# Gates of a PEER layer: one-hot products on TensorE, or a scatter into device memory and a multiply on VectorE

## The chip, the cores and the metric

One core of a Trainium2 chip runs the whole program in one launch. The metric is device time in microseconds from start to end of that launch; lower is better. The engines are TensorE (PE; PEld is its weight load), VectorE (DVE), ScalarE (ACT), GpSimd (POOL) and SyncE (SP), which issues most DMAs. A trailing q (SPq, POOLq) is an engine's own queue of instructions.

## What is computed

A decoder trunk of two layers over 256 tokens of width 1024. Layer 0 is a Mamba2-SSD mixer and then a PEER block, layer 1 an HGRN2 mixer and then a PEER block, with RMSNorms before each and at the end. The change is in the PEER block:

```python
def one_block(xb):                          # 128 tokens
    q = (xb @ w_query).reshape(nb, 8, 2, 128)
    sc = jnp.einsum('nhcd,hckd->nhck', q, sub_keys)
    top_s, top_i = lax.top_k(sc, 16)        # per head and half
    ...
    best_s, best_pos = lax.top_k(cand_s, 16)
    idx = jnp.take_along_axis(cand_i, best_pos, axis=-1)
    gate = jax.nn.softmax(best_s, axis=-1)
    u, v = expert_u[idx], expert_v[idx]
    act = jax.nn.gelu(jnp.einsum('nhkd,nd->nhk', u, xb), approximate=False)
    return jnp.einsum('nhk,nhkd->nd', gate * act, v)
```

There are 16384 experts, numbered i x 128 + j. Each token picks 16 of them for each of 8 heads, and the same expert may be picked by two heads of a token.

## The kernel before

Neither kernel gathers experts. Each streams all 16384 rows of expert_u and expert_v through TensorE, 128 experts a tile, in 128 tiles of 512 KB for u and 128 for v. The activations of all experts for all 256 tokens are kept in SBUF (`big`: 128 x 128 x 256), and a gate that is zero for experts not picked is multiplied in between u and v.

A stream of tiles runs through all stages of the program (ssd_in, ssd_z, ssd_out, q0, u0, v0, hgrn_in, hgrn_out, q1, u1, v1). For each tile SP loads `raw` into one of four buffers, ACT rounds it to `whi` (L465), POOL or VectorE makes the rest `wlo` = raw - whi, and TensorE multiplies hi by hi, hi by lo and lo by hi. In u (L783, `project`) these are 24 matmuls of 256 columns a tile, and ACT's Gelu moves the result to `big` (L711). In v (L1114, `contract`) they are 12 matmuls of 512 columns; the activations are split in the same way, by ACT into `hhi` (L747) and by POOL into `hlo` (L453), two tiles ahead. Before the change POOL makes `wlo` in the q and u stages (L424) and VectorE in v (L1712).

During the u stage VectorE makes the lists (L1607 to L1660): for two blocks of 128 tokens it finds the top 16 of each half, head by head, then of the 256 sums (`cand`, L1629), turns positions into indices i and j (L1648, L1652, L1655), and subtracts the best score. ACT takes the exponential, VectorE divides by the sum.

Then comes the gate stage, after the last u tile and before the first v tile. Indices were written as 7 bits of +1 and -1 plus a bias row, sent through device memory to be turned (`feat`, `feat_rows`), and multiplied with a matrix of signs (L1075, `matches`): a sum is positive only where i or j agrees. ACT and VectorE turn the sums into one-hot rows (`oha`, L736; `ohb`, weighted by the gate, L1698 and L741), TensorE multiplies them for each token (L1094), which gives the 128 x 128 table of gates of that token, and VectorE multiplies eight tokens' tables into `big` (L1689). 32 such rounds make a layer. `clear` (L819) writes zeros to the four banks in which v accumulates.

The order on each engine is that of the code. All waits are on semaphores: ACT's split of tile g waits until TensorE is done with tile g - 4, SP's load waits until `wlo` of the tile four before is made, and TensorE waits for both parts of a tile. The loads of v's tiles after the second wait for the end of the gate stage, since `ohb` lies in `raw`.

Of the kernel before, what the change touches and what calls it, by code (L numbers as in the profile page):

```python
# [28 lines left out]
P = 128  # L29
# [17 lines left out]
BITS = 7  # L47
FEAT = BITS + 1

# [4 lines left out]

ON_DVE = ("ssd_in", "hgrn_in", "hgrn_out", "v0", "v1")
# [5 lines left out]
for _n, _c in STREAM:  # L61
    FIRST[_n], POOL_LO[_n], DVE_LO[_n], EVAC[_n] = _g, _p, _d, _e
    _g += _c
    if _n in ON_DVE:
        _d += _c
    else:
        _p += _c
    if _n not in ("ssd_out", "v0", "v1"):
        _e += _c
# [33 lines left out]
LISTS_AT = 24  # L103


def trunk(nc, x_t, par, con, w_dt, weights, sub_keys, out_t):
# [11 lines left out]
    with ctx:  # L118
# [12 lines left out]
        zero = sb("zero", [P, 512], mybir.dt.bfloat16)  # L131
        gate_t = sb("gate_t", [P, T])
        signs = sb("signs", [P, 16, P], BF16)
# [22 lines left out]
        def norm_bank(n):  # L156
# [15 lines left out]
        ones_set = sem("ones_set")  # L172

# [71 lines left out]
        gate_v = sem("gate_v")  # L245
        lt_mm = sem("lt_mm")
        lt_v = sem("lt_v")
        oha_done = sem("oha_done")
        ohb_done = sem("ohb_done")
        ohb_act = sem("ohb_act")  # L250
        xa_mm = sem("xa_mm")
        xb_mm = sem("xb_mm")
        signs_mm = sem("signs_mm")
        signs_v = sem("signs_v")
        feat_v = sem("feat_v")
        feat_out = sem("feat_out")
        feat_in = sem("feat_in")
        gate_mm = sem("gate_mm")
# [68 lines left out]
        oha = [hhi[:, 2 * r:2 * r + 2, :].rearrange("p a (b k) -> p (a b) k", k=P) for r in range(4)]  # L327
        ohb = [raw[:, 2 + r, :, :] for r in range(2)]
        whole = work(26112, 512, 4).bitcast(U32)
        feat = work(26624, 2048).bitcast(BF16).rearrange("p (c f k) -> p c f k", c=4, f=FEAT)  # L330
        feat_rows = small[:, :, :].rearrange("p a b -> p (a b)").bitcast(BF16) \
            .rearrange("p (s k) -> p s k", s=32)
        feat_out_t = [nc.dram_tensor(f"feat{n}", [4, P, FEAT, P], BF16).ap() for n in range(2)]

# [13 lines left out]
        def rounds(eng, name, body, first=True, last=False):  # L348

            n = COUNT[name] // RAW  # L350
            a, b = int(first), n - int(last)
            if first:
                body(0)
            if b > a:
                with eng.Fori(a, b) as i:
                    body(i)
            if last:
                body(n - 1)

# [3 lines left out]
        def _(sp):  # L363
# [5 lines left out]
            sp.dma_start(tri, con[CON["tri"]]).then_inc(tri_in, 16)  # L369

# [7 lines left out]

            prev = None
            for name in STAGES:  # L380
                lo, at = (lo_dve, DVE_LO) if name in ON_DVE else (lo_pool, POOL_LO)
# [5 lines left out]
                def body(i):  # L387
                    for r in range(RAW):
                        if isinstance(i, int) and i == 0:
                            before = None  # L390
                            if prev is not None:
                                plo, pat = (lo_dve, DVE_LO) if prev in ON_DVE else (lo_pool, POOL_LO)
                                before = plo, pat[prev] + COUNT[prev] - RAW + r + 1
                            if name[0] == "v" and r == 2:

                                sp.wait_ge(gate_mm, 32 * int(name[1]) + 32)
                        else:
                            before = lo, at[name] + RAW * i + r - RAW + 1
                        load(name, i, r, before)
                if name == "hgrn_in":  # L400

                    body(0)
                    sp.wait_ge(x_done, 8)
                    sp.dma_start(lev, con[CON["lev"]:NCON].rearrange("n p q -> p n q")).then_inc(lev_in, 16)
                    with sp.Fori(1, COUNT[name] // RAW) as i:
                        body(i)
                else:
                    rounds(sp, name, body)
                prev = name
# [7 lines left out]
        def _(pool):  # L417
# [9 lines left out]
            def los(name, a=0):  # L427
                with pool.Fori(a, COUNT[name] // RAW) as i:  # L428
                    for r in range(RAW):
                        lo(name, i, r)  # L430

            for layer in range(2):
                if layer == 0:
                    los("ssd_z")
                    los("ssd_out")
# [7 lines left out]
                los(f"q{layer}")  # L443
                los(f"u{layer}")
# [14 lines left out]
        def _(act):  # L459
# [161 lines left out]
            for layer in range(2):  # L621
# [90 lines left out]
                stream(f"u{layer}", gelu, 0, SCRATCH0 // RAW)  # L712

                act.wait_ge(lists, 2 * layer + 2)
                nc.scalar.activation(lst[:, 2, :], lst[:, 2, :], ACT.Exp).then_inc(gexp, 1)
                nc.scalar.preload_act_table(ACT.Gelu)
                act.wait_ge(feat_v, layer + 1)
                act.dma_start(feat_out_t[layer].rearrange("c t f k -> t c f k"), feat).then_inc(feat_out, 16)
                stream(f"u{layer}", gelu, SCRATCH0 // RAW, 26)

                act.wait_ge(lt_v, layer + 1)
                act.wait_ge(feat_out, 16 * layer + 16)
                for c in range(2):
                    act.dma_start(feat_rows[64 * c:64 * c + 64], feat_out_t[layer][2 * c:2 * c + 2]
                                  .rearrange("b (s t) f k -> (t f) (b s) k", t=8)).then_inc(feat_in, 16)
                stream(f"u{layer}", gelu, 26)

                for m in range(32):  # L730
                    if m >= 2:

                        act.wait_ge(gate_mm, 32 * layer + m - 1)
                    for q in range(2):
                        act.wait_ge(xa_mm, 64 * layer + 2 * m + q + 1)
                        nc.scalar.activation(oha[2 * (m % 2) + q], bank[4 + q].rearrange("p (n k) -> p n k", n=4),  # L736
                                             ACT.Relu).then_inc(oha_done, 1)
                    act.wait_ge(ohb_done, 32 * layer + m + 1)
                    for t in range(6, 8):
                        a = 8 * m + t  # L740
                        ins = nc.scalar.activation(ohb[m % 2][:, t, :], bank[7][:, P * (t - 4):P * (t - 3)],  # L741
                                                   ACT.Relu, scale=gate_t[:, a:a + 1])
                    ins.then_inc(ohb_act, 1)

                def c_hi(j, r):

                    nc.scalar.activation(hhi[:, r, :], col(j), ACT.Copy).then_inc(chi, 1)  # L747
                act.wait_ge(gated, 32 * layer + 32)
# [24 lines left out]
        def _(pe):  # L773
# [14 lines left out]
            def tile_ready(name, i, r):  # L788
                g = FIRST[name] + RAW * i + r
                pe.wait_ge(hi_done, g + 1)  # L790
                if name in ON_DVE:
                    pe.wait_ge(lo_dve, DVE_LO[name] + RAW * i + r + 1)
                else:
                    pe.wait_ge(lo_pool, POOL_LO[name] + RAW * i + r + 1)

            def project(name, a=0, b=None, rs=None):

                def body(i, rs=range(RAW)):
                    for r in rs:
                        tile_ready(name, i, r)  # L800
# [16 lines left out]
            def clear():  # L817
                for b in range(4, 8):
                    nc.tensor.matmul(bank[b][:, :], zero[:, 0:P], zero[:, :], start=True, stop=True,  # L819
                                     skip_group_check=True)  # L820
# [11 lines left out]
            pe.wait_ge(signs_v, 1)  # L832
            nc.tensor.transpose(bank[5][:, 0:P], var[:, 0:P], ident[:, :]).then_inc(signs_mm, 1)
# [122 lines left out]
            for layer in range(2):  # L956
# [98 lines left out]
                project(f"u{layer}", 0, LISTS_AT)  # L1055

                pe.wait_ge(sc_a, 8 * layer + 8)
                pe.wait_ge(gate_v, layer + 1)
                for b in range(NB):
                    ins = nc.tensor.transpose(bank[4][:, P * b:P * (b + 1)], lst[:, 2, b * P:(b + 1) * P],  # L1060
                                              ident[:, :])
                ins.then_inc(lt_mm, 1)
                project(f"u{layer}", LISTS_AT)


                pe.wait_ge(evac, EVAC[f"u{layer}"] + 128)

                pe.wait_ge(feat_in, 32 * layer + 32)

                def matches(m):  # L1070

                    for c in range(2):
                        for q in range(2):
                            u = 2 * c + q
                            nc.tensor.matmul(bank[4 + u], feat_rows[32 * u:32 * u + 32, m, :],  # L1075
                                             signs[32 * u:32 * u + 32, 4 * u:4 * u + 4, :], start=True,
# [723 lines left out]
```

## Time and profile before

| | us |
|---|---|
| median of 2 runs (2211.09 to 2212.76) | 2211.93 |
| span of the profiled execution | 2208.8 |
| TensorE busy in that span | 2105.6 |
| VectorE busy | 1168.0 |
| ACT busy | 1092.3 |
| POOL busy | 1163.2 |

The span runs from the first to the last instruction of one execution under the profiler; the 3.1 us up to the median lie around it. Busy times of engines overlap, so they don't add up to the span. Times in the rows further down are counted from the start of the span, and durations of matmuls overlap, since they are pipelined.

### The profile page before, as it was taken

To read this page: it belongs to the slowest core of one execution; us is meant where nothing else is said; L and a number is where in the kernel's file an instruction comes from. 1 tells how busy PE (TensorE), PEld (TensorE's weight loads), DVE (VectorE), ACT (ScalarE), POOL (GpSimd) and SP (SyncE) were. 2 spreads that over 40 slices of the span, in tenths; PEclk is the share of its full clock that TensorE was granted. 3 is DMA by queue.
4 is the path that set the end of the run, shared out by engine and by line. 5 is a ranking of instruction groups with operands and counts; after the bars stand their busy time and mean duration, and the time that the engine had idled before them with its cause. 6 is when DMAs were issued, how large, how long until landed. Compare 5 with 4: busy or idle time off the path is not lost.

```text
span 2208.8 us, 42003 instructions
## 1 busy us (share of the span) xinstructions
PE 2105.6 (95%) x14527; PEld 1937.3 (88%) x14530; DVE 1168.0 (53%) x1838; ACT 1092.3 (49%) x1651; POOL 1163.2 (53%) x584
## 2 busy tenths in 40 slices
PE   6986999999999999999999989999999999999998
PEld 5985899999999878888889979999999987888886
DVE  5867459990001854444448944999100086444444
ACT  4654444445445655455455344444544465544553
POOL 0162668898885045554530007889788603455452
PEclk9998999999999999999999989999999999999999
DMA  4541545556563056666645334555657404665663
GB/s 142 162 124 58 165 141 179 174 170 191 188 195 119 1 173 193 195 191 192 195 145 168 98 115 153 162 172 170 190 186 196 141 1 153 191 195 193 191 192 101
DMA packets 103889, 345.74 MB, mean 157 GB/s; under 512 B 18704, under 2 KB 20240, under 8 KB 103440
## 3 DMA queue, kind: packets, MB, share of 16 engines
q1 hardware_dynamic: 94512, 340.67, 49.4%
q10 hardware_dynamic: 9312, 4.19, 1.0%
q8 instruction: 41, 0.67, 0.1%
q14 instruction: 24, 0.20, 0.0%
HBM read 341.68 MB, written 3.15 MB: 156 GB/s over the span
## 4 chain that ended last, share of the span: by engine, by line
PE 49%; issue 29%; POOL 21%; DVE 1%; POOLq 0%; ACT 0%; DVEq 0%; ACTq 0%
PE banks L1114 32%; POOL wlo L424 20%; PE banks L783 10%; PE banks L1094 6%; PE banks L1075 1%; POOLq L428 0%; POOLq L423 0%; PE banks L826 0%; DVE x L1724 0%; DVE big L1150 0%; DVE big L1719 0%; DVE big L1689 0%; POOL hlo L453 0%; DVE raw L1698 0%; POOL big L438 0%
## 5 line engine op out<-in xcount | busy, mean ns | idle before, releaser
L424 POOL TENSOR_TENSOR wlo<-raw,whi 128x1024 fp32r<-128x1024 f32 x320 | 807.2, 2532 | 502.5 <-ACT whi L465 501.5
L783 PE MATMUL banks<-hhi,whi 128*128 128x256 f32 x3072 | 881.0, 287 | 41.1 <-POOL wlo L424 16.6
L465 ACT ACTIVATE whi<-raw 128x1024 fp32r<-128x1024 f32 x640 | 675.1, 1057 | 448.6 <-PE banks L1114 338.8
L783 PE MATMUL banks<-hlo,whi 128*128 128x256 f32 x3072 | 873.5, 284 | 0.0
L783 PE MATMUL banks<-hhi,wlo 128*128 128x256 f32 x3072 | 873.2, 284 | 0.0
L783 PEld LDWEIGHTS banks<-hhi,whi 128*128 128x128 f32 x3072 | 593.2, 193 | 48.6 <-issue 25.9
L453 POOL TENSOR_TENSOR hlo<-big,hhi 128x256 fp32r<-128x256 f32 x256 | 351.9, 1375 | 505.8 <-ACT hhi L747 505.8
L783 PEld LDWEIGHTS banks<-hlo,whi 128*128 128x128 f32 x3072 | 593.4, 193 | 0.2
L783 PEld LDWEIGHTS banks<-hhi,wlo 128*128 128x128 f32 x3072 | 592.9, 193 | 0.0
L1712 DVE TENSOR_TENSOR wlo<-raw,whi 128x1024 fp32r<-128x1024 f32 x256 | 315.5, 1233 | 371.5 <-ACT whi L465 371.4
L1114 PE MATMUL banks<-whi,hhi 128*128 128x512 f32 x1024 | 316.8, 391 | 4.5 <-POOL hlo L453 4.5
L1114 PE MATMUL banks<-whi,hlo 128*128 128x512 f32 x1024 | 316.5, 390 | 0.0
L1114 PE MATMUL banks<-wlo,hhi 128*128 128x512 f32 x1024 | 316.2, 390 | 0.0
L711 ACT ACTIVATE big<-banks 128x256 f32 x256 | 98.4, 385 | 394.5 <-PE banks L783 394.4
L1114 PEld LDWEIGHTS banks<-whi,hhi 128*128 128x128 f32 x1024 | 192.9, 189 | 45.6 <-issue 5.4
L1114 PEld LDWEIGHTS banks<-wlo,hhi 128*128 128x128 f32 x1024 | 192.9, 188 | 40.3
L1114 PEld LDWEIGHTS banks<-whi,hlo 128*128 128x128 f32 x1024 | 192.9, 188 | 40.1
L1698 DVE SCALAR_TENSOR_TENSOR raw<-banks,gate_t 128x768 f32<-128x768 f32 x64 | 61.3, 958 | 190.6 <-PE banks L1075 190.5
L1094 PEld LDWEIGHTS banks<-raw,hhi 128*128 128x128 f32 x1024 | 123.7, 191 | 18.4 <-issue 14.0
L1094 PE MATMUL banks<-raw,hhi 128*128 128x128 f32 x1024 | 137.2, 287 | 2.5 <-DVE raw L1698 2.5
L747 ACT ACTIVATE hhi<-big 128x256 fp32r (+1 forms) x256 | 102.1, 399 | 5.5 <-DVE big L1689 5.5
L736 ACT ACTIVATE hhi<-banks 128x512 fp32r<-128x512 f32 x128 | 69.5, 595 | 47.0 <-PE banks L1075 47.0
(241 smaller groups left out, 1343.0 us busy)
## 6 DMA issues: line engine op xcount, KB each, us to landing
raw<-w_u SPq DMA_DIRECT2D x256, 512.0 KB, 3.5
raw<-w_v SPq DMA_DIRECT2D x256, 512.0 KB, 4.0
raw<-w_ssd_in SPq DMA_DIRECT2D x40, 512.0 KB, 3.6
raw<-w_q SPq DMA_DIRECT2D x32, 512.0 KB, 3.7
raw<-w_hgrn_in SPq DMA_DIRECT2D x32, 512.0 KB, 4.3
raw<-w_ssd_out SPq DMA_DIRECT2D x16, 512.0 KB, 3.9
raw<-w_hgrn_out SPq DMA_DIRECT2D x8, 512.0 KB, 3.6
big<-keys SPq DMA_DIRECT2D x2, 1024.0 KB, 6.5
```

The costliest lines, as they stand in the source:

```text
L424: nc.gpsimd.tensor_tensor(wlo[:, r, :, :], raw[:, r, :, :], whi[:, r, :, :].bitcast(F32), ALU.subtract).then_inc(lo_pool, 1)
L453: nc.gpsimd.tensor_tensor(hlo[:, r, :], big[:, bass.ds(j, 1), :].rearrange("p a b -> p (a b)"), hhi[:, r, :].bitcast(F32), ALU.subtract).t ...
L465: nc.scalar.activation(whi[:, r, :, :], raw[:, r, :, :], ACT.Copy).then_inc(hi_done, 1)
L711: nc.scalar.activation(col(t), bank[r][:, 0:T], ACT.Gelu).then_inc(evac, 1)
L736: nc.scalar.activation(oha[2 * (m % 2) + q], bank[4 + q].rearrange("p (n k) -> p n k", n=4), ACT.Relu).then_inc(oha_done, 1)
L747: nc.scalar.activation(hhi[:, r, :], col(j), ACT.Copy).then_inc(chi, 1)
L783: ins = nc.tensor.matmul(out, w[:, r, k, :], h[:, k, :], start=start and n == 0, stop=stop and n == 3 * KC - 1, **kw)
L1075: nc.tensor.matmul(bank[4 + u], feat_rows[32 * u:32 * u + 32, m, :], signs[32 * u:32 * u + 32, 4 * u:4 * u + 4, :], start=True, stop=True) ...
L1094: ins = nc.tensor.matmul(bank[2 * (m % 2) + q][:, P * t:P * (t + 1)], oha[2 * (m % 2) + q][:, t, :].bitcast(F32), ohb[m % 2][:, 4 * q + t, ...
L1114: ins = nc.tensor.matmul(bank[4 + 2 * b + e][:, :], c[:, r, tok], w[:, r, 4 * e:4 * e + 4, :], start=False, stop=True, skip_group_check=True)
L1698: nc.vector.scalar_tensor_tensor(out=ohb[m % 2][:, 0:6, :], in0=banks[:, 6:8, :].rearrange("p a (n k) -> p (a n) k", n=4)[:, 0:6, :], scal ...
L1712: nc.vector.tensor_tensor(wlo[:, r, :, :], raw[:, r, :, :], whi[:, r, :, :].bitcast(F32), ALU.subtract).then_inc(lo_dve, 1)
```

## The change

The gate stage on TensorE goes, with all that fed it. In its place:

- Two tables of 128 x 128 x 256 fp32 in device memory (16.8 MB each) take the gates, ordered as v's tiles need them. SP writes zeros into the first beside the loads of ssd_in, ssd_z, ssd_out and q0 (64 DMAs of 256 KB), and into the second beside those of hgrn_in (32 of 512 KB).
- POOL scatters the gates: for each layer 256 indirect DMAs, each of one number from each of 128 partitions, which add it to the table at an offset that VectorE worked out (`places`). They go in waves of 16, one wave a head and block: within a wave no two write the same place, and a wave waits until the one before has landed.
- POOL makes `wlo` for the first 24 tiles of u only (`U_POOL`), VectorE for the other 104: four at the end of block 0's lists, 40 between the steps of block 1's (`fill`), the rest in a loop. The gates of block 0 are finished after the first head of block 1 (`gates(0)`), so POOL's waves begin there.
- SP loads the table back as 128 tiles of 128 KB into four buffers (`g_ring`), the first four after the last two waves have landed, and each further one ahead of a load of v. VectorE multiplies tile j + 2 into `big` right after making `wlo` of v's tile j, and ACT's `hhi` of a tile waits for that multiply.

The core of the diff:

```diff
+U_POOL = 24
...
-                los(f"u{layer}")
+                los(f"u{layer}", U_POOL)
+
+                pool.wait_ge(zeroed[layer], 16 * (64 if layer == 0 else 32))
+                for w, (la, b, h) in enumerate(waves):
+                    if la != layer:
+                        continue
+                    if h == 0:
+                        pool.wait_ge(offs_v, NB * layer + b + 1)
+                    else:
+                        pool.wait_ge(*spread_at(w - 1))
+                    for k in range(TOPK):
+                        n = b * P + h * TOPK + k
+                        nc.gpsimd.indirect_dma_start(
+                            out=g_rows[layer], out_offset=bass.IndirectOffsetOnAxis(ap=offs[:, n:n + 1], axis=0),
+                            in_=lst[:, 2, n:n + 1], in_offset=None,
+                            compute_op=ALU.add).then_inc(spread[w % 2], 16)
...
+            def gate_load(layer, i, r):
+                j = RAW * i + r
+                if not isinstance(i, int) or i:
+                    sp.wait_ge(gated, 128 * layer + j - RAW + 1)
+                sp.dma_start(g_ring[:, r, :], g_tiles[layer][j]).then_inc(g_in[r], 16)
...
+                    if name[0] == "v":
+                        for w in (16 * layer + 14, 16 * layer + 15):
+                            sp.wait_ge(*spread_at(w))
+                        for r in range(RAW):
+                            gate_load(layer, 0, r)
...
+                def places(b):
+                    cols = slice(b * P, (b + 1) * P)
+                    row = small[:, 5, 0:P]
+                    step(nc.vector.tensor_scalar(row, lst[:, 0, cols], float(T), token[:, b:b + 1], ALU.mult, ALU.add))
+                    step(nc.vector.scalar_tensor_tensor(out=offs[:, cols], in0=lst[:, 1, cols], scalar=float(P * T),
+                                                        in1=row, op0=ALU.mult, op1=ALU.add))
...
+                        fill(2 * b)
+                        if b and h == 0:
+                            gates(0)
...
-                for m in range(32):
-                    dve.wait_ge(xb_mm, 64 * layer + 2 * m + 2)
...
-                multiply(31)
+                gate_tile(0, 0)
+                gate_tile(0, 1)
...
+                    for r in range(RAW):
+                        v_lo(i, r)
+                        gate_tile(i, r, 2)
```

Three places in the order of the instructions. On POOL, between the loop over u's tiles (`wlo`) and the loop over v's (`hlo`); before:

```order
L428 COMPARE_AND_BRANCH
L455 UNCONDITIONAL_BRANCH
L455 ISA
L453 ISA
L453 TENSOR_TENSOR hlo<-big,hhi 128x256
```

and now:

```order
L478 COMPARE_AND_BRANCH
L507 DMA gates<-small 4194304x1 x256
L521 UNCONDITIONAL_BRANCH
L521 ISA
L519 ISA
L519 TENSOR_TENSOR hlo<-big,hhi 128x256
```

The 256 indirect DMAs of a layer stand ahead of every `hlo` of v; nothing else moved on POOL, and the loop ahead of them runs 6 times instead of 32.

On VectorE, one head of block 1's lists (`cand` is the 128x256 sum, in `big`); before:

```order
L1614 MAX big<-big 128x8 x2
L1617 MAX_INDEX big<-big 128x8 x2
L1629 TENSOR_TENSOR big<-big 128x256
L1607 MAX small<-big 128x8
L1610 MAX_INDEX big<-small,big 128x8
L1611 MATCH_REPLACE big<-small,big 128x256
L1614 MAX small<-big 128x8
L1617 MAX_INDEX big<-small,big 128x8
```

and now, for the first head:

```order
L1606 TENSOR_TENSOR wlo<-raw,whi 128x1024 x2
L1645 TENSOR_TENSOR big<-big 128x256
L1592 MAX small<-big 128x8
L1595 MAX_INDEX big<-small,big 128x8
L1596 MATCH_REPLACE big<-small,big 128x256
L1599 MAX small<-big 128x8
L1602 MAX_INDEX big<-small,big 128x8
L1606 TENSOR_TENSOR wlo<-raw,whi 128x1024 x2
L1629 TENSOR_REDUCE small<-small 128x8
L1630 RECIPROCAL small<-small 128x8
L1631 TENSOR_TENSOR small<-small 128x128
```

Two splits of u tiles stand ahead of the sum and two behind the head's last step; the three rows at the end are block 0's gates, which stand behind the first head alone.

On SP, where the loads of u end and those of v begin; before:

```order
L376 DMA raw<-w_u 128x1024
L355 REGISTER_ALU
L355 COMPARE_AND_BRANCH
L376 DMA raw<-w_v 128x1024 x4
L355 UNCONDITIONAL_BRANCH
```

and now:

```order
L370 DMA raw<-w_u 128x1024
L448 REGISTER_ALU
L448 COMPARE_AND_BRANCH
L370 DMA raw<-w_v 128x1024 x4
L384 DMA small<-gates 128x256 x4
L457 UNCONDITIONAL_BRANCH
L457 ISA
L384 ISA
L384 DMA small<-gates 128x256
L369 REGISTER_ALU
L370 ISA
L370 DMA raw<-w_v 128x1024
```

Four loads of gate tiles (into `small`, where `g_ring` lies) stand behind v's first four, and one more ahead of each later load of v; the wait for the last waves stands ahead of the first of them, so v's fifth load is queued behind it.

## Rows read from the trace of the kernel before

**Rows 1.** The page, part 1: busy us, share of span, instructions.

```profile
PE 2105.6 (95%) x14527; PEld 1937.3 (88%) x14530; DVE 1168.0 (53%) x1838; ACT 1092.3 (49%) x1651; POOL 1163.2 (53%) x584
```

**Rows 2.** Windows: u, gates and v of both layers; start of hgrn_in.

```profile
core 0: us, PE busy (x) PEld busy (x) DVE busy (x) ACT busy (x) POOL busy (x), PEclk, DMA share, GB/s
324.90:705.80 380.90, 371.67 (x3081) 369.50 (x3079) 164.78 (x429) 178.72 (x262) 319.64 (x126) 1.00 0.57 176
705.80:787.30 81.50, 77.85 (x644) 65.47 (x645) 70.54 (x66) 53.96 (x130) 1.26 (x2) 1.00 0.02 8
787.30:1139.00 351.70, 350.23 (x1538) 289.52 (x1539) 159.52 (x131) 175.77 (x257) 175.23 (x127) 1.00 0.63 192
1380.30:1760.90 380.60, 371.61 (x3077) 369.43 (x3075) 167.24 (x429) 178.63 (x261) 318.93 (x126) 1.00 0.58 177
1760.90:1842.40 81.50, 77.79 (x643) 65.39 (x644) 70.45 (x66) 54.16 (x131) 1.19 (x2) 1.00 0.03 8
1145.00:1190.00 45.00, 45.00 (x357) 44.59 (x356) 28.27 (x38) 27.34 (x32) 0.70 (x2) 0.98 0.53 175
```

**Rows 3.** Chain of waits: start us, us, what; u, last gate multiply, v.

```profile
641.59 63.62 PE banks L783 x528
...
784.18 1.23 DVE big L1689
...
787.26 350.07 PE banks L1114 x1536
```

**Rows 4.** Timeline: start us, us, row; program start, first u matmul, first match.

```profile
11.25 6.68 PE L826 MATMUL banks<-big,ones 128*128 128x256 f32 x16 [1.57 <-ACT big L497]
...
324.93 0.36 PE L783 MATMUL banks<-hhi,whi 128*128 128x256 f32 x1
...
705.77 0.39 PE L1075 MATMUL banks<-signs,small 32*128 32x512 bf16 x4 [0.58 <-ACT big L711]
```

**Rows 5.** Timeline of VectorE, lists of layer 0: heads, then one index half.

```profile
322.27 0.49 DVE L1607 MAX8 big<-big 128x8 f32<-128x128 f32 x2 [1.60 <-ACT big L704]
...
397.44 0.49 DVE L1607 MAX8 big<-big 128x8 f32<-128x128 f32 x2
...
403.03 0.47 DVE L1607 MAX8 big<-big 128x8 f32<-128x128 f32 x2
...
443.66 4.37 DVE L1648 TENSOR_TENSOR big<-big,iota 128x2048 f32<-128x2048 f32 x1
448.06 4.38 DVE L1652 TENSOR_TENSOR big<-big 128x2048 f32<-128x2048 f32 x1
452.48 2.29 DVE L1655 TENSOR_REDUCE small<-big 128x128 f32<-128x2048 f32 x1
```

**Rows 6.** Single lines: ns min/median/max, first and last start, forms.

```profile
L1629 DVE TENSOR_TENSOR big<-big x32: 424/431/2587, 325.1 to 1498.0; 128x256 f32<-128x256 f32 x32
...
L1712 DVE TENSOR_TENSOR wlo<-raw,whi x256: 1218/1226/1746, 785.3 to 2182.8; 128x1024 fp32r<-128x1024 f32 x128
...
L453 POOL TENSOR_TENSOR hlo<-big,hhi x256: 1076/1372/1726, 786.0 to 2183.2; 128x256 fp32r<-128x256 f32 x128
```

**Rows 7.** DMA: an issue on SP; queues; issues with KB and us to landing.

```profile
1.20 0.42 SPq L365 DMA_DIRECT2D pars<-par  x1
...
q1 hardware_dynamic: 94512, 340.67, 49.4%
q10 hardware_dynamic: 9312, 4.19, 1.0%
...
raw<-w_u SPq DMA_DIRECT2D x256, 512.0 KB, 3.5
raw<-w_v SPq DMA_DIRECT2D x256, 512.0 KB, 4.0
...
out_t<-big SPq DMA_DIRECT2D x2, 512.0 KB, 2.7
```

More of the change, by code:

```diff
@@ L46 @@
 TOPK = 16
-BITS = 7
-FEAT = BITS + 1
 RAW = 4
@@ L172, in trunk @@
         ones_set = sem("ones_set")
+        zeroed = [sem(f"zeroed{n}") for n in range(2)]
         sq_done = sem("sq_done")
@@ L244, in trunk @@
         gexp = sem("gexp")
[L245 to L258, printed above, removed]
+        offs_v = sem("offs_v")
+        spread = [sem(f"spread{n}") for n in range(2)]
+        g_in = [sem(f"g_in{r}") for r in range(RAW)]
         gated = sem("gated")
@@ L324, in trunk, with spread_at, lo_at @@
         halff = work(tkw + 1920, 256, 2)
[L327 to L333, printed above, removed]
+        g_dram = [nc.dram_tensor(f"gates{n}", [KEYS * P * T], F32).ap() for n in range(2)]
+        g_rows = [g.rearrange("(n c) -> n c", c=1) for g in g_dram]
+        g_tiles = [g.rearrange("(j p t) -> j p t", p=P, t=T) for g in g_dram]
+        g_zero = [g.rearrange("(n p c) -> n p c", p=P, c=ZCOLS) for g in g_dram]
+        g_ring = small[:, 4:8, :]
+        offs = small[:, 3, :].bitcast(U32)
+        gsum = work(25088, PH)
+        gtop = work(25088 + PH, PH)
+        waves = [(la, b, h) for la in range(2) for b in range(NB) for h in range(PH)]
+        def spread_at(w):
+            return spread[w % 2], (w // 2 + 1) * TOPK * 16
+        def lo_at(name, t):
+            if name in ON_DVE:
+                return lo_dve, DVE_LO[name]
+            if name[0] == "u" and t >= U_POOL:
+                return lo_dve, DVE_LO[name] - U_POOL
+            return lo_pool, POOL_LO[name]
         def level_bank(n, b):
@@ L385, in _, with first @@
                     sp.dma_start(sk, sub_keys[int(name[1])]).then_inc(keys_in, 16)
-                def body(i):
+                layer = int(name[1]) if name[0] == "v" else 0
+                def first():
                     for r in range(RAW):
[L389 to L396, printed above, removed]
-                        else:
-                            before = lo, at[name] + RAW * i + r - RAW + 1
-                        load(name, i, r, before)
@@ new lines, in zeros @@
+                def zeros(i):
+                    for r in range(RAW):
+                        if name == "hgrn_in":
+                            clear_gates(1, 2 * (RAW * i + r), 2)
+                        else:
+                            a, _, at = zeros_at[name]
+                            clear_gates(0, RAW * (i - a) + at + r)
+                first()
+                n = COUNT[name] // RAW
+                if name in zeros_at:
+                    a, b, _ = zeros_at[name]
+                    if a == 0:
+                        zeros(0)
+                    with sp.Fori(1, b) as i:
+                        body(i, 1)
+                        zeros(i)
+                    if b < n:
+                        with sp.Fori(b, n) as i:
+                            body(i, 1)
+                elif name == "hgrn_in":
@@ new lines, in _, with gate_tile @@
+                    if b == 0:
+                        fill(4)
+                    places(b)
+                assert tc[0] == TK_STEPS, tc
+                assert filled_to[0] <= SCRATCH0, filled_to
+                fill(SCRATCH0 + 2 - filled_to[0])
+                gates(1)
+                fill(2)
+                with dve.Fori(filled_to[0] // RAW, COUNT[f"u{layer}"] // RAW) as i:
+                    for r in range(RAW):
+                        u_lo(RAW * i + r, r)
+                def gate_tile(i, r, ahead=0):
+                    j = RAW * i + r + ahead
+                    r = (r + ahead) % RAW
+                    dve.wait_ge(g_in[r], 4 * (j - r) + 16 + 512 * layer)
+                    v = big[:, bass.ds(j, 1), :].rearrange("p a b -> p (a b)")
+                    nc.vector.tensor_tensor(v, v, g_ring[:, r, :], ALU.mult).then_inc(gated, 1)
@@ L1714, in _ @@
+                for r in range(RAW):
+                    v_lo(n - 1, r)
+                    if r < 2:
+                        gate_tile(n - 1, r, 2)
                 if layer == 0:
```

256 lines of the change are left out of this document (99 added, 157 removed).

## Prediction

> **What bounds the kernel now.** First read the page's busy shares: TensorE is busy 95% of the span, the other engines about half [rows 1]. A share is an average, so next the windows by stage [rows 2]. [...] Then the chain of waits [rows 3]: 528 matmuls of the u stage in a row take 63.62 us, so a u tile of 24 matmuls takes 2.89 us and 128 tiles 370 us; 1536 matmuls of v take 350 us, 2.735 us a tile. The u stage of 381 us is thus 370 us of matmuls and some 11 us of gaps. TensorE's timeline gives the ends of the gate stage: u begins at 324.93, the first match matmul at 705.77 [rows 4], and v starts at 787.26, 1.85 us after the end of the last gate multiply [rows 3]. So TensorE is the bound, and whatever leaves it is won if nothing else is late.
>
> **What goes.** The match and gate matmuls, with the one-hot work of ACT and VectorE and the multiplies that they feed, are 81.5 us in each layer [rows 2]. Without any new wait, v could start when the last u tile is evacuated, one gate tile is multiplied (0.43 us, a two-input VectorE operation of 128x256 [rows 6]), and the 1.85 us of splitting have passed. The features and their trip through memory were off TensorE's path; the sign matrix at the start was too, since TensorE's first sums wait for ACT's squares there [rows 4]. I count nothing for either.
>
> **The u stage on VectorE.** POOL now splits 24 tiles instead of 128, VectorE the other 104. VectorE's timeline [rows 5] puts the first block's top-16 work between 322.27 and 397.44; 24 tiles at 2.89 us carry TensorE from 324.93 to 394.3, so a few us are lost there at most. In the second block one head took 5.57 us (397.44 to 403.03); with four splits of 1.23 us [rows 6] and their gaps it takes 10.7 us, and TensorE needs 11.56 us for four tiles. The index part takes 4.37 + 4.38 + 2.29 us a half [rows 5]; two of these operations last twice the reduction of the same 2048 columns, which I put down to POOL's reads beside them, so with POOL relieved the half is 7 to 11 us plus 5.1 us of splits, against 11.56 us. VectorE therefore keeps up within a few us. I take 370 + 6 us for the stage: TensorE's u work ends near 701. Bounds: 0 and 25 us of stall.
>
> **The scatter, which decides.** Each layer issues 256 indirect DMAs on POOL, in 16 waves of 16; each wave waits until the one before has landed. SP loads the first gate tiles after the last wave, and v cannot start earlier. So POOL's chain counts from the first gates to the last landing. It begins when VectorE has finished block 0 (397.44), four splits (5.1 us), the addresses (under 1 us), the next head (10.7 us) and the gates (1 us): at about 415. The second block's gates are ready near tile 74, at 325 + 74 x 2.89 + 6 = 545, before block 0's eight waves end, and hold nothing up. A wave costs 16c + L, with c the time POOL needs for one DMA and L the time from the last issue to its landing. Then v starts at 415 + 16 x (16c + L) + 5.8, where 5.8 us are the gate loads (3.5 us to land [rows 7]), the multiply and the 1.85 us.
>
> No row of this trace shows an indirect DMA, so I bound. For c: SP issues a plain DMA in 0.42 us, and the shortest DMA here lands in 2.7 us, which is what each would cost if POOL could not go on sooner [rows 7]. The ends are far apart. The row nearest in kind is POOL's shortest operation that reads and writes SBUF in the v stage, 1076 ns [rows 6]; I take c = 1.08 us (the geometric mean of the ends, 1.07, agrees). For L: 2.7 us for a store and 3.5 to 4.0 us for the loads that run beside it; I take 3.5 us, being in the same stage as the u loads [rows 7]. A wave is then 16 x 1.08 + 3.5 = 20.8 us, sixteen are 333 us, the chain ends at 748 and v starts at 753 or 754. That is 34 us earlier than 787.26. Of the 83.8 us that v could have gained (start at 703.5), 50 are handed back as a new wait of TensorE. Each tenth of a us in c is 25.6 us a layer: the whole prediction hangs on this row.
>
> [...]
>
> **Gate tiles in v.** Per tile VectorE gets 1.23 + 0.43 us against 2.735 us of matmuls: hidden. The loads add 128 packets of 1 KB. Page part 3 gives 185 ns for a weight packet (49.4% of 16 engines over 94512) and 38 ns for those of the short queue [rows 7]; by bytes between, 65 ns, so 128 x (185 + 65) / 16 = 2.0 us of 2.735: hidden. If a 1 KB packet cost as much as a weight packet it would be 2.96 us, and 29 us a layer lost: the other bound.
>
> **Clearing.** 16.8 MB of zeros per layer go out beside weight loads. The tightest place is the start of hgrn_in: its tiles run at TensorE's pace [rows 2], and a round of four moves 2.1 MB of weights and 2.1 MB of zeros in 11.6 us. Part 3 gives 3605 bytes in 185 ns, so 16 engines move 312 GB/s: 13.4 us a round, three such rounds. I take 5 us for both layers together; bounds 0 and 15.
>
> **Sum.** Two layers of 34 us less, 5 us more: 63 us. The profiled execution spans 2208.8 us and the median of the runs is 3.1 us above; that rest stays. 2211.9 - 63 = 2149 us.
>
> **Rivals.** First, the scatter is hidden: c below 0.89 us. Then v starts at 703.5, and 2 x 83.8 - 5 = 163 us are won: 2049 us. For it: POOL has nothing else to do then, and SP's issue of 0.42 us. Against: 128 addresses have to be computed from a table, which SP never does.
>
> Second, an even trade: c between 1.12 and 1.29 us, where the new wait eats the gate stage. At c = 1.20 it is 2212 us.
>
> Third, slower: VectorE's splits hold POOL up. In v a POOL operation has a shortest of 1076 ns and a median of 1372 beside VectorE's splits [rows 6], so a two-input operation of VectorE costs POOL 0.30 us. If every indirect DMA, which must read its offsets, pays that, c is 1.38 us, the chain ends at 824, v starts at 830, 43 us later than now: 2211.9 + 86 + 5 = 2303 us. It turns slower from 0.21 us a DMA on. If DMAs ran only in the 57% of a tile that a split leaves free, c would be 1.89 and the time 2564. Against it: the median of the cand sum beside POOL is its minimum (431 and 424 ns [rows 6]), so the two often miss each other.
>
> [...]
>
> **Numbers.** Forecast (c from 0.89 to 1.12): 0.33. Hidden: 0.14. Even: 0.18. Slower, by the third rival or simply a dearer DMA: 0.35. A change over 2% is about what a measurement of this kernel tells from none. Faster 0.47, same 0.18, slower 0.35. Since cases of both signs hold most of the chance, the range is wide: 2040 (hidden, clearing free) to 2430 (c = 1.63). The forecast's own range is 2049 to 2168.
>
> **What would show it.** In the new profile TensorE should wait 45 to 55 us per layer between the last u matmul and the first v matmul, with the gate loads as releaser and POOL's DMA queue full from 415 to 748. If that gap is 3 us, the first rival holds; if it exceeds 81 us, the third. Waits of u matmuls on VectorE's splits should stay under 25 us a layer, v at 350 us, and hgrn_in's waits on its loads under 15. The forecast is wrong if a wave takes under 18 or over 21.5 us.

## The result, and the profile after

The changed kernel takes 2966.66 us (median of 2 runs, 2963.81 to 2969.52) against 2211.93: 1.342 times as long, 95% interval 1.3394 to 1.3445. The forecast was 2149, the range ended at 2430. The change is slower by 755 us, and its sign was missed too.

The page of the kernel after, part 1 and one row of part 3 (queue, kind: packets, MB, share of 16 engines), answers to [rows 1, 7]:

```profile
PE 1950.7 (66%) x13242; PEld 1807.6 (61%) x13245; DVE 1422.6 (48%) x2140; ACT 991.2 (33%) x1401; POOL 1478.7 (50%) x888
...
q0 software_dynamic: 73728, 0.29, 7.3%
```

TensorE has 155 us less to do than before, and its share has fallen from 95% to 66%. No engine took its place: VectorE and POOL are about half busy. When nobody is busy, somebody waits, so next come the windows by stage (the columns are those of [rows 2]): u, the stretch behind it and v of layer 0, the start of hgrn_in, and the stretch of layer 1.

```profile
324.90:704.00 379.10, 373.40 (x3095) 371.38 (x3094) 253.92 (x535) 182.71 (x267) 213.40 (x105) 1.00 0.64 175
704.00:1168.00 464.00, 0.00 (x0) 0.00 (x0) 2.29 (x4) 1.70 (x3) 270.28 (x175) 0.50 0.17 2
1168.00:1519.00 351.00, 350.51 (x1536) 289.79 (x1536) 268.29 (x256) 173.38 (x254) 172.07 (x128) 0.99 0.75 237
1527.00:1572.00 45.00, 44.22 (x356) 43.60 (x355) 28.77 (x38) 27.43 (x32) 0.23 (x2) 1.00 0.95 361
...
2144.00:2595.00 451.00, 0.00 (x0) 0.00 (x0) 2.46 (x4) 1.78 (x3) 263.19 (x170) 0.50 0.17 2
```

Where the gate stage had 81.5 us, TensorE now stands still for 466 and 459 us (two waits, 925.8 us in the row of waits below; the windows of the two stretches begin 3 and 9 us after TensorE stopped). Nearly all the work there is POOL's. V and the start of hgrn_in are as long as before to within 1 us, and u is 6 us shorter, although VectorE has 89 us more in u and 109 us more in v. The first and the last matmul of u:

```profile
326.85 0.36 PE L828 MATMUL banks<-hhi,whi 128*128 128x256 f32 x1
...
700.76 0.28 PE L828 MATMUL banks<-hhi,wlo 128*128 128x256 f32 x1
```

That is 374 us from start to end, where it was 380 before (324.93 in [rows 4] to 705.2). The granted clock is 1.00 in u, 0.50 in the idle stretch and back at 0.99 in the v stage behind it, which takes the 351 us it took before.

TensorE's and VectorE's waits (engine line waited for: us, times, longest), and the end of the chain of waits in layer 0:

```profile
PE banks L1113 <- POOL hlo L519: 925.8, 2, 466.4
...
DVE big L1702 <- DMA small<-gates: 933.8, 2, 470.6
```

```profile
1160.46 2.97 DMA gates<-small
1163.50 2.12 DMA small<-gates
1168.33 350.52 PE banks L1113 x1536
```

TensorE's wait is put down to POOL's split of the first gated tile, which is only the last link: VectorE waits 470 us for the first gate tile, that load waits for the last indirect DMA to land (1160.46 + 2.97 = 1163.4), and that DMA was late because POOL came to it only at 1160.46. So the scatter is on the path for its whole length, from POOL's first DMA at 420.70 on. POOL's timeline of one wave in the idle stretch (start us, us, then in brackets the idle time before and what ended it), and the line of the indirect DMAs in the u stage and behind it, up to 1160 us:

```profile
783.82 1.55 POOL L507 DMA_INDIRECT gates<-small  x1 [1.80 <-DMA gates<-small]
785.68 1.55 POOL L507 DMA_INDIRECT gates<-small  x1 [0.30 <-issue]
787.53 1.55 POOL L507 DMA_INDIRECT gates<-small  x1 [0.30 <-issue]
791.08 1.55 POOL L507 DMA_INDIRECT gates<-small  x1 [2.00 <-issue]
...
822.97 1.55 POOL L507 DMA_INDIRECT gates<-small  x1 [1.98 <-issue]
```

```profile
L507 POOL DMA_INDIRECT gates<-small x80: 1546/1626/3442, 420.7 to 695.1; - x80
its engine sat idle before it (us, times) until:
  issue: 117.3, 75
...
DMA to landing us min/median/max: 3.0/4.3/5.9
```

```profile
L507 POOL DMA_INDIRECT gates<-small x175: 1546/1548/1567, 699.1 to 1157.0; - x175
...
  issue: 172.1, 165
...
DMA to landing us min/median/max: 2.9/3.0/3.2
```

Three things stand in these rows. One DMA keeps POOL busy for 1.55 us and the next follows 0.30 us later: 1.85 us, not 1.08. After seven of the sixteen, always the third, sixth, seventh, ninth, twelfth, fourteenth and fifteenth of a wave, POOL pauses for some 1.6 us more, with no releaser in the profile. And the five waves that run beside the u stage start at 420.70, 480.56, 537.59, 590.61, 647.53 and the sixth at 699.08: 52 to 60 us each, where the later ones take 42.3 in the mean (they start at 741.24, 783.82, 824.82 and so on).

### The profile page after: what moved, and what is told of

Its sections match the earlier page's. It is cut to its first block, busy times and chain, and to the rows that moved or that the text cites. A ratio compares the mean times of both kernels' runs of the same rounds, so it can differ in the third digit from the quotient of the medians.

```text
span 2962.0 us, 41122 instructions
## 1 busy us (share of the span) xinstructions
PE 1950.7 (66%) x13242; PEld 1807.6 (61%) x13245; DVE 1422.6 (48%) x2140; ACT 991.2 (33%) x1401; POOL 1478.7 (50%) x888
## 3 DMA queue, kind: packets, MB, share of 16 engines
q0 software_dynamic: 73728, 0.29, 7.3%
## 4 chain that ended last, share of the span: by engine, by line
issue 37%; POOL 34%; PE 25%; DMA 4%; DVE 1%; ACT 0%; POOLq 0%; ACTq 0%; DVEq 0%; SPq 0%
POOL gates L507 27%; PE banks L1113 24%; POOL wlo L474 7%; DMA gates<-small 3%; PE banks L828 1%; DVE wlo L1606 0%; DMA small<-gates 0%; PE banks L870 0%; DVE x L1733 0%; POOL hlo L519 0%; DVE big L1149 0%; DVE big L1728 0%; POOLq L478 0%; ACT whi L531 0%; POOL big L488 0%
## 5 line engine op out<-in xcount | busy, mean ns | idle before, releaser
L507 POOL DMA_INDIRECT gates<-small x512 | 836.3, 1633 | 686.4 <-issue 580.4
L1113 PE MATMUL banks<-whi,hhi 128*128 128x512 f32 x1024 | 317.3, 391 | 925.8 <-POOL hlo L519 925.8
L1702 DVE TENSOR_TENSOR big<-big,small 128x256 f32 (+1 forms) x256 | 242.9, 949 | 933.8 <-DMA small<-gates 933.8
L474 POOL TENSOR_TENSOR wlo<-raw,whi 128x1024 fp32r<-128x1024 f32 x112 | 290.1, 2610 | 409.7 <-ACT whi L531 409.4
L1712 DVE TENSOR_TENSOR wlo<-raw,whi 128x1024 fp32r<-128x1024 f32 x256 | 314.6, 1229 | 153.4 <-ACT whi L531 153.2
L1606 DVE TENSOR_TENSOR wlo<-raw,whi 128x1024 fp32r<-128x1024 f32 x208 | 253.7, 1223 | 217.4 <-ACT whi L531 217.1
L1400 DVE TENSOR_TENSOR wlo<-raw,whi 128x1024 fp32r<-128x1024 f32 x32 | 39.0, 1221 | 13.9 <-ACT whi L531 13.9
```

What stands on the lines that cost most here:

```text
L474: nc.gpsimd.tensor_tensor(wlo[:, r, :, :], raw[:, r, :, :], whi[:, r, :, :].bitcast(F32), ALU.subtract).then_inc(lo_pool, 1)
L507: nc.gpsimd.indirect_dma_start(out=g_rows[layer], out_offset=bass.IndirectOffsetOnAxis(ap=offs[:, n:n + 1], axis=0), in_=lst[:, 2, n:n + 1 ...
L1113: ins = nc.tensor.matmul(bank[4 + 2 * b + e][:, :], c[:, r, tok], w[:, r, 4 * e:4 * e + 4, :], start=False, stop=True, skip_group_check=True)
L1400: nc.vector.tensor_tensor(wlo[:, t % RAW, :, :], raw[:, t % RAW, :, :], whi[:, t % RAW, :, :].bitcast(F32), ALU.subtract).then_inc(lo_dve, 1)
L1606: nc.vector.tensor_tensor(wlo[:, r, :, :], raw[:, r, :, :], whi[:, r, :, :].bitcast(F32), ALU.subtract).then_inc(lo_dve, 1)
L1702: nc.vector.tensor_tensor(v, v, g_ring[:, r, :], ALU.mult).then_inc(gated, 1)
```

## The experiments

**Without the scatter, and where it stands.** The first run prices all that is not the scatter; SP waits for the zeros and the offsets in place of the last waves.

```diff
-                    for k in range(TOPK):
-                        nc.gpsimd.indirect_dma_start(
...
-                        for w in (16 * layer + 14, 16 * layer + 15):
-                            sp.wait_ge(*spread_at(w))
```

> This kernel leaves out all 512 indirect DMAs, so v multiplies by zeros; everything else of the change is there. Theory (the scatter is the whole loss, the rest is as the prediction had it): v starts about 3 us after the u stage ends, and the time is 2966.7 less the two idle stretches of 464 and 451 us, 2050 to 2065 us. Rival (the other parts, the splits on VectorE, the gate tiles or the clearing, cost too, hidden by the long wait): over 2100 us.

It took 2039.8 us (2212.6 for the kernel before in the same runs). From its chain of waits and its windows:

```profile
542.33 155.78 PE banks L811 x1296
701.27 350.05 PE banks L1096 x1536
```

```profile
324.90:698.10 373.20, 369.63 (x3066) 368.24 (x3066) 250.92 (x521) 180.29 (x262) 60.82 (x22) 1.00 0.55 179
701.20:1051.00 349.80, 349.73 (x1536) 289.44 (x1536) 267.91 (x255) 173.28 (x253) 173.46 (x127) 1.00 0.73 238
```

U ends at 698.1 and v starts 3.2 us later; the time is 10 us under what was expected, mostly because 915 us were taken off for the idle stretches, and the two waits come to 925.8. U takes 374 us with and without the scatter beside it. So the rest of the change is worth 173 us, and the scatter costs 927 (2966.7 - 2039.8). The loads of gates and the second multiply cost v nothing.

**Half the DMAs in each wave** tells a price per DMA from a price per wave.

```diff
-                    for k in range(TOPK):
+                    for k in range(TOPK // 2):
```

> Eight of the sixteen indirect DMAs in each wave, still 16 waves; half the gates are left out. Theory (each DMA costs POOL its own 1.85 to 3.45 us, about 2.4 in the mean, and the landing little): a wave alone takes 20 to 22 us instead of 42.3, one beside the u stage 25 to 30, v starts near 836 and the time is about 2300 us. Rival (a wave has a large fixed price, its landing and the wait for it): a wave alone stays over 30 us and the time over 2600. The steps of 3.45 us should come after the same places 2, 5 and 6 if they belong to the column of the offsets, and at places that alternate from wave to wave if they go by the position in a ring or in the program.

The kernel took 2280.6 us, near the 2300 of the theory. A wave alone took 21.0 us, its start and the next one's in this timeline:

```profile
733.89 1.55 POOL L507 DMA_INDIRECT gates<-small  x1 [1.68 <-DMA gates<-small]
...
751.81 1.55 POOL L507 DMA_INDIRECT gates<-small  x1 [1.93 <-issue]
755.00 1.55 POOL L507 DMA_INDIRECT gates<-small  x1 [1.65 <-DMA gates<-small]
```

Half of 42.3: the price is per DMA. The pauses come after the third, sixth and seventh of every wave (places 2, 5 and 6 counted from 0), so they don't go by a count that runs on; each wave begins them anew. That leaves two readings, something in the columns of the offsets, or room that is free again when a wave has landed, and this run doesn't tell them apart.

**A write in place of the add** asks who sets the pace.

```diff
-                            in_=lst[:, 2, n:n + 1], in_offset=None,
-                            compute_op=ALU.add).then_inc(spread[w % 2], 16)
+                            in_=lst[:, 2, n:n + 1], in_offset=None).then_inc(spread[w % 2], 16)
```

> The indirect DMAs write instead of adding (a key that two heads choose keeps only one gate). Theory (POOL's making of the addresses sets the pace, not what the DMA engines do with them): a wave alone stays at 42 us, the time within 1% of 2967. Rival (the read of the old value before each add holds up the queue): waves under 35 us, the time under 2750.

2366.4 us: the theory as I had put it fell. The rival's numbers came, with a wave alone at 24.2 us; its reason, the read of the old value, isn't shown by that, since more than the read goes with the add (POOL's busy time and the packets, in the rows here). From its timeline (first, seventh, eighth DMA of a wave, and the next wave's first), and its queue:

```profile
714.36 0.95 POOL L507 DMA_INDIRECT gates<-small  x1 [1.42 <-DMA gates<-small]
...
721.92 0.96 POOL L507 DMA_INDIRECT gates<-small  x1 [0.30 <-issue]
724.65 0.96 POOL L507 DMA_INDIRECT gates<-small  x1 [1.77 <-issue]
...
738.60 0.96 POOL L507 DMA_INDIRECT gates<-small  x1 [1.44 <-DMA gates<-small]
```

```profile
q0 software_dynamic: 16384, 0.29, 0.5%
```

POOL is busy 0.96 us with a write and 1.55 with an add, and pauses twice in a wave instead of seven times. The queue shows why both could be: 512 adds make 73728 packets, 144 each, and 512 writes 16384, 32 each. One reading is that POOL's own time goes with what it writes out for the DMA engines, and that the pauses are a place that fills up. The second half is tested below, the first is not.

**All waves behind u** tests whether the first waves are long because of what runs beside them.

```diff
+                pool.wait_ge(evac, EVAC[f"u{layer}"] + 128)
                 pool.wait_ge(zeroed[layer], 16 * (64 if layer == 0 else 32))
```

> POOL starts the first wave only when the u stage is over, so all 16 waves run beside idle engines. Theory (what runs in the u stage, VectorE first of all, makes its five waves of a layer 50 to 60 us instead of 42.3): all 16 waves take 42.3 us, v starts 683 us after the end of u in both layers, and the time is about 3415 us. Rival (the first waves are slow for being first, whatever runs beside them): the first five waves again take 50 to 60 us, and the time is over 3500.

3384.9 us, 3415 expected. All 512 DMAs are now like those of the undisturbed waves, and sixteen of these lie between the end of u at 699 and the start of v at 1375 (the line of the DMAs; the chain):

```profile
L508 POOL DMA_INDIRECT gates<-small x512: 1542/1548/1669, 699.9 to 3007.7; - x171
```

```profile
1374.85 350.45 PE banks L1114 x1536
```

675 us from the end of u to v, 683 expected. So the company in the u stage lengthens the waves, not their being first.

**Eight times the scratch size** tests the pauses. The last lines of the kernel set `dynamic_dma_scratch_size=1024`. I take this number for room for what POOL writes out for its DMAs, the descriptors of the expectations; no row shows what is kept there, and what can be measured is the pauses and the time at another value.

```diff
-    nc = bacc.Bacc("TRN2", target_bir_lowering=False, num_devices=1, dynamic_dma_scratch_size=1024)
+    nc = bacc.Bacc("TRN2", target_bir_lowering=False, num_devices=1, dynamic_dma_scratch_size=8192)
```

> [...] Theory (the pauses of 1.6 us after fixed places, seven in a wave of adds and two in a wave of plain writes, are POOL waiting for room among the descriptors it has written): with eight times the room the pauses go, a wave alone takes 15 x 1.85 + 3.3 = 31 us instead of 42.3 and one beside the u stage 30 to 36, v starts near 935 and the time is near 2500 us. Rival (the pauses belong to something else, such as the fetching of the program or the reading of the offsets): waves and time stay, 42 us and 2967.

2568.9 us: 398 us back for one number. POOL's timeline behind u (first, second and last DMA of a wave, the next wave's first), and the line of the DMAs beside u:

```profile
746.11 1.55 POOL L507 DMA_INDIRECT gates<-small  x1 [1.72 <-DMA gates<-small]
747.97 1.55 POOL L507 DMA_INDIRECT gates<-small  x1 [0.30 <-issue]
...
773.92 1.55 POOL L507 DMA_INDIRECT gates<-small  x1 [0.30 <-issue]
777.14 1.55 POOL L507 DMA_INDIRECT gates<-small  x1 [1.67 <-DMA gates<-small]
```

```profile
L507 POOL DMA_INDIRECT gates<-small x112: 1546/1674/3047, 418.5 to 679.2; - x112
```

The pauses are gone, all of them, and a wave alone takes 31.0 us, as expected. Beside u a wave takes 34 to 41 us, a little over the 30 to 36 expected, and seven such waves a layer make up the 69 us by which the time missed 2500 (418.5 to 683.3 is 265 us, 33 each would be 231). So the pauses go with this number, and the columns of the offsets, which are the same here, are out. That POOL waited for room is my reading of it: the result fits it, and no row shows the room itself. The pauses are gone beside u too, where all the loads of u still run (32.0 us of idle time with no releaser before 105 of the 112 DMAs, 0.30 each): what is left there is POOL's busy time, 30.5 us for the sixteen DMAs of a wave in the mean instead of 24.8, and up to 2.4 us at a wave's end.

**What in the u stage slows the waves.** My theory was VectorE, as in the third rival of the prediction. Three runs put one kind of work each into the idle stretch from 704 on: 200 subtractions, 200 copies, or a stream of copies between places in device memory.

```diff
+                for i in range(200):
+                    nc.vector.tensor_tensor(wlo[:, i % 2, :, :], ab[0], ab[1], ALU.subtract).then_inc(busy, 1)
```

> The kernel after, with 200 more subtractions of 128x1024 on VectorE (two inputs, the u stage's own operation, 1.23 us each) back to back from the end of the u stage on, into a buffer that nobody reads. Theory (VectorE's two-input operations slow POOL's indirect DMAs): the five or six waves that run beside them take 50 us or more instead of 42.3, the later ones 42.3 again, and the time grows by 80 to 200 us. Rival (the weight loads of the u stage slow them): all waves after u stay at 42.3 us and the time at 2967.

```diff
+                    nc.vector.tensor_copy(wlo[:, i % 2, :, :], ab[0]).then_inc(busy, 1)
```

> As the run before it, with copies (one input) in place of subtractions. If only two-input operations disturb POOL, the waves stay at 42.3 us and the time at 2967; if any VectorE work does, they lengthen as with the subtractions.

```diff
+                        for i in range(100):
+                            sp.dma_start(spare[i % 2], weights[name][4 + i % 2, :, :]).then_inc(filler[i % 2], 16)
```

> The kernel after, with 100 copies of 0.5 MB from one place of device memory to another, issued by SP from the end of the u stage on, two in flight, to give the DMA engines the load they have in the u stage or more. Theory (VectorE, not the loads, makes the waves beside u long): waves beside the copies take at most 46 us. Rival: 50 us or more.

They took 2997.7, 2974.9 and 3088.6 us. The line of the indirect DMAs in the first 120 us of each, in the order subtractions, copies on VectorE, copies in memory:

```profile
L508 POOL DMA_INDIRECT gates<-small x40: 1546/1958/2635, 707.7 to 823.5; - x40
...
  issue: 39.4, 38
```

```profile
L508 POOL DMA_INDIRECT gates<-small x41: 1657/1899/2151, 706.0 to 823.4; - x41
...
  issue: 41.0, 39
```

```profile
L516 POOL DMA_INDIRECT gates<-small x32: 1546/1556/1567, 706.7 to 820.4; - x32
...
  issue: 59.0, 30
```

The second line of each is the idle time before the DMAs with no releaser (us, times). Under the subtractions, with VectorE busy throughout, a wave takes 46 to 50 us, under its copies 46 to 47: 3 to 8 us more than alone, by a longer busy time (median 1.96 and 1.90 us instead of 1.55) with the pauses as they were. That is less than the theory had (50 us or more) and more than its rival had (42.3). Under the copies in memory a wave takes 56 to 61 us: the busy time stays at 1.55, and the idle time before a DMA goes from 1.04 us in the mean (172.1 over 165 above) to 1.97 (59.0 over 30). So the last theory fell, and its rival holds: DMA load by itself lengthens a wave by 14 to 19 us. It acts by way of the pauses, since at 8192 none is left beside the same loads of u. DMAs also land later there (4.3 us in u, 3.0 behind it), which fits room that is free again later; no run tests that link by itself.

How the two divide in the u stage can be read from the trace of the kernel after. Its window from the start of the first wave to that of the sixth:

```profile
420.70:699.08 278.38, 278.23 (x2318) 277.92 (x2316) 167.29 (x283) 134.01 (x197) 148.25 (x81) 1.00 0.70 183
```

Five waves took 278.4 us, 67 more than five alone. POOL is busy 148 us of it, where 80 DMAs of 1.55 us are 124: 24 us. The idle time with no releaser is 117.3 us over 75 DMAs, where 75 x 1.04 are 78: 39 us. The last 4 us lie at the waves' ends. So of the 13 us by which a wave is longer some 8 are pauses, which DMA load lengthens, and 5 are busy time (3 to 7, wave by wave), which VectorE's work lengthens and copies in memory don't; whether another engine of the u stage has a part in the 5 was not tried. VectorE's part doesn't need two inputs: its copies, with one input and 0.65 us each where a subtraction takes 1.21, do it too. An indirect DMA took POOL 1.96 us beside the subtractions and 1.55 alone; in which part of POOL's work on a DMA the 0.41 us lie, the reading of the offsets or another, isn't told apart here. The copies in memory are a heavier load than the u stage (DMA share 0.79 against 0.70), so they show the kind of the effect and not its exact share.

**A kernel that beats both.** The runs so far say what a scatter may be: at 8192 a wave takes 34 to 41 us beside u, and from 418 to the end of u at 699 there are 280 us, enough for seven waves and not for sixteen. So the scatter takes the first 128 tokens, eight waves, and the one-hot stage of before the other 128, in 16 rounds of 8 tokens instead of 32. The table has half the size, and the scratch size is 4096. Its core:

```diff
-        waves = [(la, b, h) for la in range(2) for b in range(NB) for h in range(PH)]
+        waves = [(la, 0, h) for la in range(2) for h in range(PH)]
...
+                matches(0)
+                for m in range(16):
...
-                    v = big[:, bass.ds(j, 1), :].rearrange("p a b -> p (a b)")
+                    v = big[:, bass.ds(j, 1), 0:HALF].rearrange("p a b -> p (a b)")
...
-    nc = bacc.Bacc("TRN2", target_bir_lowering=False, num_devices=1, dynamic_dma_scratch_size=1024)
+    nc = bacc.Bacc("TRN2", target_bir_lowering=False, num_devices=1, dynamic_dma_scratch_size=4096)
```

> [...] Theory (a wave of adds beside the u stage takes 34 to 41 us where there is room for its descriptors, so eight of them hide, 16 do not): the waves end near 418 + 8 x 38 + 3 = 725 us, beside u and the gate stage, which has 16 x 2.55 = 41 us from 704 on; v starts near 748 instead of 787.3, in each layer 39 us earlier, and the time is 2125 to 2145 us. Rival (the scatter is still not done when the gate stage ends, or the two disturb each other): TensorE waits again for the loads of gates, v starts at 770 or later and the time is over 2175 us.

2121.5 us (median of 4 runs) against 2210.2 for the kernel before beside it: a ratio of 0.960, 95% interval 0.9586 to 0.9619. Its windows u, gate stage, v of layer 0:

```profile
324.90:698.80 373.90, 370.29 (x3072) 368.75 (x3070) 255.22 (x537) 180.76 (x263) 276.05 (x136) 1.00 0.65 177
698.80:742.70 43.90, 39.38 (x324) 32.82 (x324) 36.67 (x37) 27.88 (x68) 23.59 (x17) 1.00 0.22 27
742.70:1093.00 350.30, 350.04 (x1536) 289.38 (x1536) 251.41 (x256) 174.43 (x255) 170.13 (x127) 1.00 0.69 215
```

The last indirect DMA of layer 0 is issued at 725.3, seventeen us before the shorter gate stage ends, and TensorE doesn't wait for it. At 4096 one pause is left in a wave, after the fifteenth add:

```profile
692.14 2.13 POOL L538 DMA_INDIRECT gates<-small  x1 [1.78 <-issue]
```

V starts 44.5 us earlier than in [rows 3], 39 expected, mostly because u ended at 698.8, where 704 had been assumed; the time is a little under the lower end of what was expected for that reason.

The same kernel with the old scratch size shows that the larger one is needed:

```diff
-    nc = bacc.Bacc("TRN2", target_bir_lowering=False, num_devices=1, dynamic_dma_scratch_size=4096)
+    nc = bacc.Bacc("TRN2", target_bir_lowering=False, num_devices=1, dynamic_dma_scratch_size=1024)
```

> [...] Theory: five waves end by 699 as in the kernel after, three more of 43 us by 828, v starts near 833 and the time is near 2305 us. Rival (the room for descriptors matters little where only eight waves run): within 20 us of the run before.

2292.8 us, 2305 expected. V waits for the scatter again, and starts at 829 in its chain (833 expected):

```profile
829.07 350.39 PE banks L1201 x1536
```

## Why the prediction was wrong, step by step

**What held.** TensorE was the bound, and u without the gate stage ends where it was put (near 701; the last u matmul of the kernel after starts at 700.76). The 376 us for u were 374, so the fills on VectorE were sized well. Two of the index operations on VectorE lasted 4.37 us before, which the prediction put down to POOL's reads beside them; with POOL relieved of the splits they last as long as the reduction, with the scatter beside them (here) and in the run without it, which bears that out:

```profile
499.84 2.29 DVE L1667 TENSOR_TENSOR big<-big,iota 128x2048 f32<-128x2048 f32 x1
```

V kept its 350 us with the gate tiles in it, and the bound of 29 us a layer for their packets is out. The clearing was taken at 5 us; without the scatter the kernel came in at 2039.8 where the "hidden" rival had 2049. Of the 9 us some 4 are v's start (701.27 instead of 703.5, in two layers), and the rest is the clearing, of which nothing shows. POOL's chain began at 420.7 instead of 415. The falsifier worked as written: the gap exceeds 81 us, and a wave is over 21.5. Two small slips of the working change nothing: 397.44 to 403.03 is 5.59 us and not 5.57, and c = 1.20 gives 2210 us and not 2212.

**The step that failed** is "I take c = 1.08 us", with the wave of 16c + L = 20.8 us that rests on it. In layer 0 the sixteen waves last from 420.7 to 1163.4, 743 us where 333 were forecast. The 410 us between are these, from the runs:

| term, layer 0 | forecast | measured | us |
|---|---|---|---|
| from one add to the next (1.55 busy + 0.30), 256 of them | 1.08 | 1.85 | +197 |
| pauses, a wave (42.3 - 31.0) | 0 | 11.3 | +181 |
| five waves beside u (278.4 - 5 x 42.3): pauses and busy time | 0 | 67 | +67 |
| from the last issue of a wave to the next wave's first, beyond the 1.85 | 3.5 | 1.4 | -34 |

They add to 411; with POOL's chain beginning 5 us late, v starts 415 us later than forecast. So the mechanism was right as far as POOL's chain decides and L is small; the size of c was wrong, and the pauses and the company of the u stage stood at nothing in the sum. The bounds for c, 0.42 to 2.7 us, did hold 1.85, and even the 2.56 that one gets with the pauses ((42.3 - 1.4) / 16). The fault is in choosing between them: c was set by the nearest row of POOL, an elementwise operation, though an indirect DMA has little in common with it but the engine; and then the range was cut at c = 1.63, well inside the upper bound. At the upper bound the formula gives v at 415 + 16 x (16 x 2.7 + 3.5) + 5.8 = 1168, where v did start (1168.33). That is luck: 2.7 us is the landing of a plain store, and in the measured sum c is 2.56 with the pauses, L is smaller, and 67 us come from the u stage.

**What no term stood for** is the pauses that go with the scratch size. The kernel before has `dynamic_dma_scratch_size=1024` in its last lines too, but its page has no software_dynamic queue ([rows 7] are hardware_dynamic ones), so neither the diff nor the trace pointed there. At 8192, 398 of the scatter's 927 us go.

**The rivals.** Hidden and even trade are out. The third had the right sign, and its mechanism, VectorE beside POOL, exists: 0.35 to 0.41 us a DMA under continuous VectorE work, 0.30 assumed. But it is the smallest of the three costs: 24 us in layer 0, and most of the 1.85 us is there with VectorE idle.

**Left open.** Which work of the u stage besides VectorE's lengthens POOL's busy time was not tried. Whether POOL's longer time for an add comes of its 144 packets, and why an add makes 144 packets and a write 32, was not tried either. Plain writes with a larger scratch size and no waits between waves were not tried; they keep only one gate where two heads choose the same key.

## What to carry to other kernels

Indirect DMAs cost the engine that issues them time of its own for each (1.85 us on POOL here), and in waves that wait for one another they are a serial chain: multiply the count by the price first, and where no row prices it, carry the upper bound to the end of the range. Where a program sets a scratch size for its DMAs, look it up and try a larger one (8192 in place of 1024 was worth 398 us here), and look for pauses at fixed places of a burst that nobody releases. And a resource that is too slow for the whole of a task can still take the part that hides: half of the tokens by scatter and half by one-hot products beat either alone.

## What the runs showed of the hardware that was not expected

- An indirect add of 128 values of 4 bytes keeps POOL 1.55 us, a plain indirect write 0.96, each with 0.30 us to the next; the packets are 144 and 32.
- With `dynamic_dma_scratch_size=1024` POOL pauses some 1.6 us seven times in 16 adds and twice in 16 writes (1.5 us each); with 4096 once in 16 adds, after the fifteenth; with 8192 never in a wave of 16.
- Load on the DMA engines lengthens those pauses (idle time before a DMA 1.04 to 1.97 us in the mean) and not POOL's busy time; VectorE's work lengthens the busy time (1.55 to 1.90 or 1.96 us in the median) and not the pauses. With 8192 there are no pauses beside the u stage's loads either (0.30 us of idle time before a DMA).
